# The second weight sum of a seven-product (Strassen-Winograd) block: by an accumulating DMA instead of a GpSimd add

## The chip, the cores and the metric

The kernel runs on one core of one Trainium2 chip. The metric is the time of one execution on the device in microseconds (us); lower is better. Each kernel is run several times and the median is compared.

## The reference

One inference step of a four-layer network on 640 tokens (512 of a sample, 128 of a context) of width 1024. Each layer is a token mixer (gated convolution, pooling, attention, gated convolution), then a SwiGLU feed-forward part of hidden width 2816; both are modulated by vectors computed from a conditioning vector.

```python
D_MODEL, D_FF = 1024, 2816
def swiglu(h, w_in, w_out):
    g, u = jnp.split(h @ w_in, 2, axis=-1)
    return (jax.nn.silu(g) * u) @ w_out
...
for i in range(DEPTH):
    mod_p = adaln(c_ctx[None, :], ada_w[i], ada_b[i])     # (1, 1024) @ (1024, 6144), in six parts
    ...
    xp = xp + mod_p[5] * swiglu(hp, ffn_in_w[i], ffn_out_w[i])
    xs = xs + mod_s[5] * swiglu(hs, ffn_in_w[i], ffn_out_w[i])
```

All is float32.

## The kernel before

**Products.** Activations are held transposed, 128 features by 640 tokens a tile. Each float32 operand is split in two rounded parts, hi and lo, and a product is three matmuls (hi by hi, hi by lo, lo by hi). The hi part of a weight tile is written by ScalarE, the lo part (weights minus hi) by VectorE.

**Pairs of seven blocks.** A part of the feed-forward input products is not done plainly. One gate tile and one up tile of 128 outputs make a pair, and with the two halves of the 1024 inputs and the two halves of the tokens the product is a 2 by 2 by 2 block product, done with seven block products instead of eight (the scheme of Winograd's form). Each block product is 4 x 3 = 12 matmuls of 128x128 weights on 322 columns (line 806). The order of the blocks is fixed (`_order`): for pair p it is (p,1), (p-1,4), (p,5), (p,6), (p,2), (p,7), (p,3), and for the first pair of a chunk 1, 5, 2, 6, 3, 7. There are 60 such pairs, in nine chunks of 6 or 8 pairs: eight in layer 0's second chunk and six in its third, and so on in layers 1 to 3.

**The weight sums.** Four of the seven blocks have sums of weights. With G the gate tile and U the up tile, L and R the left and right halves of their inputs: block 5 is s1 = U_L + U_R, block 6 is s2 = s1 + G_L, block 3 is s4 = s2 + G_R, block 7 is s3 = U_L + G_L. Their homes are 128x512 tiles of 256 KB: s1 in `rope[:, 0]`, s2 in `rope[:, 1]`, s4 in `tmp[:, 2]`, and s3 in the up tile's own left half. Each home holds one pair's sum at a time. For pair p the steps are, with their lines:

- SP (the queue that issues plain loads): the gate and up tiles, 512 KB each (465), issued once the tiles of pair p-2 are free (VectorE's mark at 1882, behind block 4); then U_L into the s1 home (483), when VectorE has read block 5 of pair p-1 (`free(5)`) and s2 of pair p-1 has been made (482).
- GpSimd (POOL): U_R added to the s1 home by an accumulating DMA (638); G_L added to U_L by an accumulating DMA, s3 (644); s2 by a tensor_tensor add (654) when s1 has landed; s4 by a tensor_tensor add (660) when VectorE has read block 3 of pair p-1. Then the loads of modulation weights (`load_ada`, 598), 512 KB each, into one of three slots.
- ScalarE writes each block's hi part (1303) into one of four slots of `w_hi` as a block's product before it ends; VectorE writes the lo part (1878) into `w_lo`; TensorE waits for that (801).

So block (p,6) is put into its slot when block (p-1,3) is done, and TensorE comes to it three blocks later. ScalarE and VectorE work in order, and both also do the rest of the pair: ScalarE copies block 1's result (1347) and does the silu (1368), VectorE adds the partial results (1942, 1950, 1971), multiplies, and in some chunks does products of the modulation (1787), which read the tiles that `load_ada` brings.

**Around the first pair of a chunk.** The sums of pair 0 of a chunk are made while the output products of the chunk before still run (`outs_and_first_pair`). There GpSimd's queue holds: three triples of modulation loads, the four sum steps of pair 0, one more triple, and then the sums of pair 1. This order is there in four chunks. VectorE does six modulation products of each triple in these stretches.

Of the kernel before, what the change touches and what calls it, by code (L numbers as in the profile page):

```python
# [20 lines left out]
ALU = mybir.AluOpType  # L21
# [83 lines left out]
HW = HALF * P  # L105
# [64 lines left out]
def _pairs_before(layer, c):  # L170
    return LAYER_S[layer] + sum(SEVENS[FIRST_SEVEN[layer]:c])
# [19 lines left out]
def build(nc, d):  # L191
    with ExitStack() as ctx:
# [3 lines left out]
        def sem(name):  # L196
            return ctx.enter_context(nc.semaphore(name))
# [92 lines left out]
        t_hi_ready = sem("t_hi_ready")  # L290
        t_lo_ready = sem("t_lo_ready")
        s1_in = sem("s1_in")
        s1_made = sem("s1_made")
        s2_made = sem("s2_made")
        s3_made = sem("s3_made")
        s4_made = sem("s4_made")
# [118 lines left out]
        s1_home, s2_home, s4_home = rope[:, 0, 0:HW], rope[:, 1, 0:HW], tmp[:, 2, 0:HW]  # L415

        def block_source(p, m):

            j = 2 * (p % 2)
            return {1: raw[:, j, 0:HW], 2: raw[:, j, HW:2 * HW], 4: raw[:, j + 1, HW:2 * HW], 7: raw[:, j + 1, 0:HW],  # L420
                    5: s1_home, 6: s2_home, 3: s4_home}[m]

        def block_home(w, n, b):
            slot = SLOT[n][b]
            return w[:, slot // 2, slot % 2 * HW:slot % 2 * HW + HW]
# [17 lines left out]
        def _(sp):  # L443
# [17 lines left out]
            def load(q, tiles, units=range(4)):  # L461
                for j in units:

                    sp.wait_ge(w_lo_ready, 4 * q + (j - 3))
                    sp.dma_start(raw[:, j, 0:tiles * P], d["weights"][4 * q + j, :, 0:tiles * P]).then_inc(raw_in[j], 16)

            def load_pair(layer, c, q, p):

                first, place, j, qq = _pairs_before(layer, c), PLACE[SEVENS[c]], 2 * (p % 2), q + p // 2
                load(qq, KD, (j, j + 1))  # L470
                up_w = d["weights"][4 * qq + j + 1]

                def free(m):
                    if p:
                        sp.wait_ge(block_lo_ready, SEVEN * first + place[p - 1, m] + 1)
                    elif first:
                        sp.wait_ge(block_lo_ready, SEVEN * first)

                free(5)
                if first + p:  # L480

                    sp.wait_ge(s2_made, first + p)
                sp.dma_start(s1_home, up_w[:, 0:HW]).then_inc(s1_in, 16)

            sp.dma_start(cond_k[:], d["cond_k"]).then_inc(cond_k_in, 16)
            load_head(0)
# [33 lines left out]
            for layer in range(DEPTH):  # L520
# [43 lines left out]
                for c in range(FIRST_SEVEN[layer], 3):  # L564
                    for p in range(SEVENS[c]):
                        load_pair(layer, c, q, p)
                    q += SEVENS[c] // 2
                    if c < 2:
                        with sp.Fori(0, Q_OUT) as i:
                            load(i + q, KD)  # L570
                        q += Q_OUT
# [15 lines left out]
        def _(pool):  # L587
# [45 lines left out]
            def sums_of_pair(layer, c, p, q):  # L633

                first, place, j, qq = _pairs_before(layer, c), PLACE[SEVENS[c]], 2 * (p % 2), q + p // 2
                pairs, gate_w, up_w = first + p, raw[:, j, :], raw[:, j + 1, :]
                pool.wait_ge(s1_in, 16 * (pairs + 1))
                pool.dma_start(s1_home, d["weights"][4 * qq + j + 1, :, HW:2 * HW], accum_op=ALU.add).then_inc(s1_made, 16)
                pool.wait_ge(raw_in[j], 16 * qq + 16)
                pool.wait_ge(raw_in[j + 1], 16 * qq + 16)  # L640
                if pairs:

                    pool.wait_ge(s3_made, 16 * pairs)
                pool.dma_start(up_w[:, 0:HW], gate_w[:, 0:HW], accum_op=ALU.add).then_inc(s3_made, 16)

                def free(m):
                    if pairs:
                        pool.wait_ge(block_lo_ready, SEVEN * first + (place[p - 1, m] + 1 if p else 0))

                pool.wait_ge(s1_made, 16 * (pairs + 1))  # L650
                free(6)
                if pairs:
                    pool.wait_ge(s4_made, pairs)
                pool.tensor_tensor(s2_home, s1_home, gate_w[:, 0:HW], ALU.add).then_inc(s2_made, 1)
                pool.wait_ge(s2_made, pairs + 1)
                free(3)
                if p == 0 and c == FIRST_SEVEN[layer]:

                    pool.wait_ge(sum_ready, 2 * layer + 2)
                pool.tensor_tensor(s4_home, s2_home, gate_w[:, HW:2 * HW], ALU.add).then_inc(s4_made, 1)  # L660

            def sums_of_chunk(layer, c, q, n):

                share = IN_ADA[layer][c] if isinstance(IN_ADA[layer][c], list) else []

                def load_for(p):
                    at, end = sum(share[:p]), sum(share[:p + 1])
                    for tile in range(-(-at // 2), -(-end // 2)):
                        load_ada(_ada_at(layer, c) + tile // ADA_N, tile % ADA_N)

                load_for(0)
                for p in range(n):
                    if p or c == 0:
                        sums_of_pair(layer, c, p, q)
                    load_for(p + 1)

            def outs_and_first_pair(layer, c, q):

                outs = OUT_ADA[layer][c]
                for i in range(sum(outs)):  # L680
                    if i == outs[0] + 1:
                        sums_of_pair(layer, c + 1, 0, q)
                    ada_triple(_ada_at(layer, c, 1) + i)
                if sum(outs) <= outs[0] + 1:
                    sums_of_pair(layer, c + 1, 0, q)
# [4 lines left out]
            for layer in range(DEPTH):  # L690
                q, kind, n = LAYER_Q[layer] + Q_MIX[KIND[layer]], KIND[layer], 2 * layer + 1
                first = FIRST_SEVEN[layer]
# [556 lines left out]
        def _(act):  # L1249
# [43 lines left out]
            def block_hi(n, b, first, q):  # L1293

                p, m = ORDER[n][b]
                if m in (1, 2):
                    act.wait_ge(raw_in[2 * (p % 2)], 16 * (q + p // 2) + 16)
                elif m == 4:
                    act.wait_ge(raw_in[2 * (p % 2) + 1], 16 * (q + p // 2) + 16)
                else:  # L1300
                    done, unit = {5: (s1_made, 16), 6: (s2_made, 1), 7: (s3_made, 16), 3: (s4_made, 1)}[m]
                    act.wait_ge(done, unit * (first + p + 1))
                act.activation(block_home(w_hi, n, b), block_source(p, m), ACT.Copy).then_inc(block_hi_ready, 1)  # L1303

            def first_blocks(layer, c, q, j):

                for b in {2: (0, 1), 3: (2, 3)}[j]:
                    block_hi(SEVENS[c], b, _pairs_before(layer, c), q)
# [22 lines left out]
            def seven_chunk(layer, c, q, n, r, g, tiles):  # L1331
# [8 lines left out]
                def refill(p, m):  # L1340
                    for b in REFILL[n][place[p, m]]:
                        block_hi(n, b, first, q)
# [412 lines left out]
        def _(dve):  # L1755
# [74 lines left out]
            def scaled_out(q, j, row, off_s=0, off_p=TS):  # L1830

                slot = j % 2
                dve.tensor_copy(bias[:, j, :], ps[:, 2 * slot + 1, T - TA:TH - TA])
                if off_p == off_s + TS:
                    v = dve.tensor_tensor(halves(row[:, off_s:off_s + T]), both(slot), halves(rinv), ALU.mult)  # L1835
                else:
                    for (_, src, dst), (_, _, r) in zip(pieces(slot, row, off_s, off_p), pieces(slot, rinv)):
                        v = dve.tensor_tensor(dst, src, r, ALU.mult)
                v.then_inc(freed[slot], 1)

                dve.wait_ge(freed[slot], evacuated(q, j))
# [818 lines left out]
```

## Time and profile before

| what | value |
|---|---|
| median of 3 runs | 2601.7 us (2601.56 to 2602.37) |
| time of the profiled execution | 2599.65 us |
| span in its profile (first to last instruction) | 2597.9 us |
| mean granted TensorE clock | 0.997 of full |
| busy: TensorE, VectorE, ScalarE, GpSimd | 99%, 79%, 39%, 21% |
| mean DMA traffic | 132 GB/s |

Busy time is the share of the span in which an engine executes; a TensorE that is busy is not necessarily at its peak. The profiled execution takes 1.75 us beyond its span, and is 2.05 us under the median of the runs.

### The profile page before, as it was taken

The page shows a single profiled execution, that of the slowest core. Times are in us where ns is not written, and L with a number is a line of the kernel's source. Part 1 is how long each engine was busy: PE and PEld are TensorE (multiplying, and loading weights), DVE is VectorE, ACT ScalarE, POOL GpSimd, SP SyncE. Part 2 cuts the span into 40 slices and gives each one's busy share as a digit, 9 for nine tenths or more (in the row PEclk, how much of TensorE's full clock was granted, in tenths as well). Part 3 has the DMA queues.
Part 4 walks back from the last instruction along what each step waited for, and adds up shares of the span by engine and source line. Part 5 has one row for each costly group of instructions (what it writes and reads, how often), then busy time and mean ns, then how long its engine had stood idle before and what let it go on. Part 6 is the DMA issues. An engine that isn't in the chain of part 4 may idle for free. (4 is left out here: it accounts for less than half of the span.)

```text
span 2597.9 us, 44163 instructions
## 1 busy us (share of the span) xinstructions
PE 2559.6 (99%) x16918; PEld 2485.7 (96%) x16918; DVE 2053.2 (79%) x3489; ACT 1010.1 (39%) x1687; POOL 548.3 (21%) x553
## 2 busy tenths in 40 slices
PE   9999999999999999999999999999999999999998
PEld 5999999999999999999976999999999998999998
DVE  5888879988786787987766788887788988858385
ACT  4223322533442222254676453442532234425253
POOL 0000243313100032330000531322200035223030
PEclk9999999999999999999999999999999999999999
DMA  7444335655423443542101255554534423545342
GB/s 299 153 139 146 124 112 180 173 186 146 139 77 129 147 154 121 184 128 96 58 13 41 78 132 188 144 166 142 147 110 145 149 102 109 160 112 141 98 134 78
DMA packets 111582, 342.83 MB, mean 132 GB/s; under 512 B 12993, under 2 KB 16193, under 8 KB 111169
## 3 DMA queue, kind: packets, MB, share of 16 engines
q1 hardware_dynamic: 68656, 216.48, 24.1%
q0 software_dynamic: 42768, 124.28, 17.8%
q8 instruction: 97, 1.59, 0.2%
q14 instruction: 61, 0.49, 0.1%
HBM read 322.09 MB, written 2.88 MB: 125 GB/s over the span
## 5 line engine op out<-in xcount | busy, mean ns | idle before, releaser
L1252 ACT ACTIVATE w_hi<-raw 128x1024 fp32r<-128x1024 f32 (+2 forms) x239 | 244.5, 1023 | 652.4 <-PE ps L754 625.1
L1787 DVE CUSTOM_DVE_ANT_0 ps_x<-ada_w,cond 128x1024 f32<-128x1024 f32 x354 | 453.2, 1280 | 20.8 <-DVE tmp L1835 3.7
L1759 DVE TENSOR_TENSOR w_lo<-raw,w_hi 128x1024 fp32r<-128x1024 f32 (+2 forms) x239 | 295.4, 1236 | 205.3 <-ACT w_hi L1252 203.8
L806 PE MATMUL ps<-turned,w_hi 128*128 128x322 f32 x1440 | 323.5, 312 | 9.4 <-DVE tmp L1971 5.7
L598 POOL DMA_DIRECT2D ada_w<-in_ada_w x177 | 95.4, 540 | 1061.2 <-DVE ada_raw L1787 1022.8
L753 PE MATMUL ps<-h_hi,w_hi 128*128 128x320 f32 x928 | 291.6, 314 | 3.0 <-DVE w_lo L1759 1.2
L754 PE MATMUL ps<-h_lo,w_hi 128*128 128x322 f32 x928 | 289.1, 311 | 0.0
L754 PE MATMUL ps<-h_hi,w_lo 128*128 128x322 f32 x928 | 288.4, 311 | 0.0
L753 PE MATMUL ps<-h_lo,w_hi 128*128 128x320 f32 x928 | 288.3, 311 | 0.0
L753 PE MATMUL ps<-h_hi,w_lo 128*128 128x320 f32 x928 | 288.2, 311 | 0.0
L754 PE MATMUL ps<-h_hi,w_hi 128*128 128x322 f32 x928 | 287.6, 310 | 0.0
L753 PE MATMUL ps<-g_hi,w_hi 128*128 128x320 f32 x884 | 274.1, 310 | 3.5 <-DVE g_lo L1773 3.5
L754 PE MATMUL ps<-g_hi,w_lo 128*128 128x320 f32 x884 | 273.2, 309 | 0.0
L753 PE MATMUL ps<-g_hi,w_lo 128*128 128x320 f32 x884 | 273.2, 309 | 0.0
L754 PE MATMUL ps<-g_lo,w_hi 128*128 128x320 f32 x884 | 273.1, 309 | 0.0
L754 PE MATMUL ps<-g_hi,w_hi 128*128 128x320 f32 x884 | 273.1, 309 | 0.0
L753 PE MATMUL ps<-g_lo,w_hi 128*128 128x320 f32 x884 | 273.1, 309 | 0.0
L1878 DVE TENSOR_TENSOR w_lo<-raw,w_hi 128x512 fp32r<-128x512 f32 x240 | 189.9, 792 | 88.8 <-ACT w_hi L1303 85.8
L806 PEld LDWEIGHTS ps<-turned,w_hi 128*128 128x128 f32 x1440 | 243.1, 189 | 11.5 <-DVE tmp L1971 7.3
L806 PE MATMUL ps<-h_hi,w_hi 128*128 128x322 f32 x720 | 226.2, 314 | 11.0 <-DVE w_lo L1878 11.0
L806 PE MATMUL ps<-h_hi,w_lo 128*128 128x322 f32 x720 | 225.3, 313 | 0.0
L806 PE MATMUL ps<-h_lo,w_hi 128*128 128x322 f32 x720 | 224.9, 312 | 0.0
(239 smaller groups left out, 6145.2 us busy)
## 6 DMA issues: line engine op xcount, KB each, us to landing
raw<-in_weights SPq DMA_DIRECT2D x323, 512.0 KB, 3.6
ada_w<-in_ada_w POOLq DMA_DIRECT2D x177, 512.0 KB, 3.6
rope<-in_weights SPq DMA_DIRECT2D x60, 256.0 KB, 3.5
rope<-in_weights POOLq DMA_DIRECT2D x60, 256.0 KB, 3.7
raw<-raw POOLq DMA_DIRECT2D x60, 256.0 KB, 4.6
raw<-in_weights SPq DMA_DIRECT2D x32, 384.0 KB, 3.2
mix<-in_ada_head SPq DMA_DIRECT2D x16, 512.0 KB, 10.5
x<-in_x SPq DMA_DIRECT2D x8, 320.0 KB, 10.1
```

Of the source, the lines that this page charges most:

```text
L598: pool.dma_start(ada_w[:, j * D:(j + 1) * D], d["ada_w"][ADA_N * qa + (j - LEAD)]).then_inc(ada_in[j], 16)
L753: pe.matmul(ps[:, 2 * slot, 0:TA], w[:, slot, ws], a(k)[:, 0:TA], start=begin, stop=end)
L754: mm = pe.matmul(ps[:, 2 * slot + 1, 0:width - TA], w[:, slot, ws], a(k)[:, TA:width], start=begin, stop=end)
L806: mm = pe.matmul(out, w[:, ws], a[:, k, :], start=begin and k == 0 and i == 0, stop=k == HALF - 1 and i == 2, skip_group_check=True)
L1252: act.activation(w_hi[:, j % 2, 0:tiles * P], raw[:, j, 0:tiles * P] if src is None else src, ACT.Copy).then_inc(w_hi_ready, 1)
L1759: dve.tensor_tensor(w_lo[:, j % 2, 0:tiles * P], raw[:, j, 0:tiles * P] if src is None else src, w_hi[:, j % 2, 0:tiles * P].bitcast(F32), ...
L1787: dve.tensor_tensor_reduce(ada_products, ada_w[:, j * D:(j + 1) * D], cond[:, v, :], 1.0, 0.0, ALU.mult, ALU.add, ada_raw[:, j, v:v + 1]). ...
L1878: dve.tensor_tensor(block_home(w_lo, n, b), block_source(p, m), block_home(w_hi, n, b).bitcast(F32), ALU.subtract).then_inc(block_lo_ready, 1)
```

## The change

The second sum s2 is no longer made by the GpSimd add of line 654. SP now loads G_L from HBM a second time, into the s2 home, with a plain DMA of 256 KB; GpSimd then issues a DMA from the s1 home to the s2 home, with accumulation, and waits for its landing before the add of s4. SP's new load stands behind the load of the s1 home, with two waits of its own: VectorE has read block 6 of pair p-1, and s4 of pair p-1 has been made. `s2_made` counts in steps of 16, as a DMA's landing does.

```diff
@@ load_pair, SP
                 if first + p:
-                    sp.wait_ge(s2_made, first + p)
+                    sp.wait_ge(s2_made, 16 * (first + p))
                 sp.dma_start(s1_home, up_w[:, 0:HW]).then_inc(s1_in, 16)
+                free(6)
+                if first + p:
+
+                    sp.wait_ge(s4_made, first + p)
+                sp.dma_start(s2_home, d["weights"][4 * qq + j, :, 0:HW]).then_inc(s2_in, 16)
@@ sums_of_pair, GpSimd
                 pool.wait_ge(s1_made, 16 * (pairs + 1))
-                free(6)
-                if pairs:
-                    pool.wait_ge(s4_made, pairs)
-                pool.tensor_tensor(s2_home, s1_home, gate_w[:, 0:HW], ALU.add).then_inc(s2_made, 1)
-                pool.wait_ge(s2_made, pairs + 1)
+                pool.wait_ge(s2_in, 16 * (pairs + 1))
+                pool.dma_start(s2_home, s1_home, accum_op=ALU.add).then_inc(s2_made, 16)
+
+                pool.wait_ge(s2_made, 16 * (pairs + 1))
                 free(3)
@@ block_hi, ScalarE
-                    done, unit = {5: (s1_made, 16), 6: (s2_made, 1), 7: (s3_made, 16), 3: (s4_made, 1)}[m]
+                    done, unit = {5: (s1_made, 16), 6: (s2_made, 16), 7: (s3_made, 16), 3: (s4_made, 1)}[m]
```

## Rows read from the trace of the kernel before

**Rows 1.** Busy time and share of the span, instructions, from the page.
```profile
PE 2559.6 (99%) x16918; PEld 2485.7 (96%) x16918; DVE 2053.2 (79%) x3489; ACT 1010.1 (39%) x1687; POOL 548.3 (21%) x553
```

**Rows 2.** Chain of waits of TensorE: releaser, us in total, times, longest.
```profile
PE ps L806 <- DVE w_lo L1878: 11.0, 5, 3.4
PE ps L806 <- DVE tmp L1971: 5.7, 6, 1.6
PE ps L806 <- ACT tmp L1347: 3.7, 2, 2.3
```

**Rows 3.** Busy time in one chunk of pairs (start:end, length, engines, clock, DMA).
```profile
core 0: us, PE busy (x) PEld busy (x) DVE busy (x) ACT busy (x) POOL busy (x), PEclk, DMA share, GB/s
2306.00:2404.00 98.00, 98.00 (x661) 98.00 (x660) 79.13 (x131) 50.40 (x97) 33.12 (x28) 1.00 0.49 132
```

**Rows 4.** Line 654: duration ns min/median/max, and who waited for it.
```profile
L654 POOL TENSOR_TENSOR rope<-rope,raw x60: 1267/1294/2366, 428.4 to 2527.1; 128x512 f32<-128x512 f32 x60
...
  ACT w_hi L1303: 4.1, 5
```

**Rows 5.** DMA issues of the page: KB each, median us to landing.
```profile
ada_w<-in_ada_w POOLq DMA_DIRECT2D x177, 512.0 KB, 3.6
rope<-in_weights POOLq DMA_DIRECT2D x60, 256.0 KB, 3.7
raw<-raw POOLq DMA_DIRECT2D x60, 256.0 KB, 4.6
```

**Rows 6.** Line 483, the load of the s1 home: its landing.
```profile
DMA to landing us min/median/max: 2.5/3.5/5.3
```

**Rows 7.** Timeline of a pair inside a chunk: start us, us, instruction, idle before.
```profile
471.51 0.33 SPq L483 DMA_DIRECT2D rope<-in_weights  x1
475.44 0.86 POOL L638 DMA_DIRECT2D rope<-in_weights  x1 [3.97 <-DMA rope<-in_weights]
475.98 1.21 POOL L644 DMA_DIRECT2D raw<-raw  x1
479.20 1.28 POOL L654 TENSOR_TENSOR rope<-rope,raw 128x512 f32<-128x512 f32 x1 [2.01 <-DMA rope<-in_weights]
480.55 1.62 POOL L660 TENSOR_TENSOR tmp<-rope,raw 128x512 f32<-128x512 f32 x1
482.21 0.63 ACT L1303 ACTIVATE w_hi<-rope 128x512 fp32r<-128x512 f32 x1 [1.15 <-PE ps L806]
484.46 0.57 PE L806 MATMUL ps<-turned,w_hi 128*128 128x322 f32 x2 [0.50 <-DVE tmp L1971]
486.71 0.68 DVE L1878 TENSOR_TENSOR w_lo<-rope,w_hi 128x512 fp32r<-128x512 f32 x1
```

**Rows 8.** Timeline of a pair whose first sum lands late.
```profile
1541.50 0.95 SPq L465 DMA_DIRECT2D raw<-in_weights  x2
1542.76 1.51 POOL L654 TENSOR_TENSOR rope<-rope,raw 128x512 f32<-128x512 f32 x1 [2.13 <-DMA rope<-in_weights]
1544.36 0.63 ACT L1303 ACTIVATE w_hi<-rope 128x512 fp32r<-128x512 f32 x1 [0.96 <-POOL rope L654]
1550.59 0.32 PE L806 MATMUL ps_sum<-h_hi,w_hi 128*128 128x322 f32 x1
```

**Rows 9.** DMA issues between 1538 and 1550 us: KB each, median us to landing.
```profile
raw<-in_weights SPq DMA_DIRECT2D x2, 512.0 KB, 5.3
raw<-raw POOLq DMA_DIRECT2D x2, 256.0 KB, 5.5
```

**Rows 10.** Timeline around the first two pairs of a chunk.
```profile
592.75 1.50 POOL L654 TENSOR_TENSOR rope<-rope,raw 128x512 f32<-128x512 f32 x1 [6.10 <-DMA rope<-in_weights]
594.33 2.17 POOL L660 TENSOR_TENSOR tmp<-rope,raw 128x512 f32<-128x512 f32 x1
596.43 1.14 POOL L598 DMA_DIRECT2D ada_w<-in_ada_w  x2
601.34 1.22 DVE L1787 CUSTOM_DVE_ANT_0 ps_x<-ada_w,cond 128x1024 f32<-128x1024 f32 x1
607.78 2.37 POOL L654 TENSOR_TENSOR rope<-rope,raw 128x512 f32<-128x512 f32 x1 [2.02 <-DMA rope<-in_weights]
609.21 2.03 DVE L1787 CUSTOM_DVE_ANT_0 ps_x<-ada_w,cond 128x1024 f32<-128x1024 f32 x1
613.86 0.39 PE L806 MATMUL ps<-h_hi,w_hi 128*128 128x322 f32 x1 [1.89 <-DVE w_lo L1878]
```

More of the change, by code:

```diff
@@ L292, in build @@
         s1_in = sem("s1_in")
+        s2_in = sem("s2_in")
         s1_made = sem("s1_made")
```

## The prediction

> **What bounds the kernel now.** I read the page's busy shares first: TensorE is busy for 2559.6 us of the span of 2597.9 [rows 1], so all its idle time together is 38 us. Next the waits by engine. Of TensorE's waits, those inside the chunks of pairs (line 806) are three rows: 11.0 us for VectorE's lo parts, 5.7 us for VectorE's line 1971, 3.7 us for ScalarE's copy [rows 2]. That is 20.4 us, and it caps what any relief of the engines around the pairs can give; the rest of the time TensorE streams. The busy time by stretch shows the pace there: 661 matmuls in 98 us with no gap [rows 3], 0.1483 us each, so a block of 12 takes 1.78 us and a pair of seven blocks 12.45 us. Whatever serves a pair in less is hidden; a cycle of loads and sums that took longer would set the pace instead.
>
> Then the timelines, to see how near the sums are to that. In a usual pair [rows 7] the s1 home is loaded at 471.51, the right half is accumulated from 475.44, s1 is there at 479.20, s2 at 480.5, and ScalarE takes s2 at 482.21: 1.7 us of room. VectorE takes it only at 486.71, since it is behind with other work. In a pair whose s1 lands late [rows 8] the room is gone: s1 is there at 1542.76, ScalarE has been waiting 0.96 us when it takes s2 at 1544.36. TensorE starts block 2 at 1550.59, so block 6 starts one block earlier, at 1548.81. The view by line says how many pairs are like this: ScalarE waited for line 654 in 5 of 60, 4.1 us [rows 4].
>
> **The part removed.** 60 adds of 1.29 us in the median [rows 4] leave GpSimd, which is busy 21% and is no bound by itself. What they cost is on VectorE: a modulation product takes 1.22 us at 601.34 with GpSimd quiet, and 2.03 us at 609.21 beside the add that began at 607.78 [rows 10]: 0.81 us lost. That counts only where TensorE then waits for VectorE. Four chunks begin with such a wait right behind the add of their second pair (the one shown is 1.89 us at 613.86; the other three are of the same kind, and these four make most of the 11.0 us [rows 2, 10]): 4 x 0.8 = 3.2 us gained. Inside the first chunk, where VectorE is never idle for long, three small waits for line 1971, the first 0.50 us long [rows 7], together 1.3 us, should vanish. The larger waits for 1971 (5.7 less 1.3, 4.4 us [rows 2]) stand beside the add of s4, which stays. Gain so far: 4.5 us.
>
> The trace agrees with the Trainium skill, SBUF — State Buffer, section Who interferes with whom, by which a VectorE instruction with two inputs in SBUF and a GpSimd instruction that reads SBUF share a read interface, and whichever starts second waits for the whole of the first. By that rule the loss next to one add could be up to the add's whole 1.29 us, and the four places would give 5.2 us and not 3.2; the row of 0.81 stands in my sum.
>
> **The part added on GpSimd.** One accumulating DMA of 256 KB from SBUF to SBUF a pair, and GpSimd waits for its landing. Its nearest relative is s3's, same size, same kind, 4.6 us in the median, but that one is issued 0.54 us behind another accumulating DMA [rows 5, 7] and lies in its queue; the one from HBM takes 3.7 [rows 5]. The new one is issued when s1 has just landed, with s3's nearly done, so without other traffic I take 4.0 us. Where SP's two loads of 512 KB fall on it, as at 1541.50 just ahead of 1542.76 [rows 8], landings are 5.3 and 5.5 us [rows 9], and I take 5.3. Bounds: 2.5 us, the least that a transfer of 256 KB took [rows 6], and 5.5 us. So s2 is made 2.7 to 4.0 us later than by the add (4.0 or 5.3 less 1.3).
>
> The Trainium skill, DMA: Bandwidth & Descriptors, section Anatomy of one DMA, gives 2.0 us plus the bytes over 436 GB/s, which is an estimate of 2.6 us here; the rows of this case, 3.7 and 4.6 us, lie above it. By 2.6 us neither late fills nor late modulation loads (below) would remain, and the sum would be the gain of 4.5 us alone; this is the first rival's condition.
>
> Who waits for s2? (a) ScalarE's fill of block 6, and in its queue behind it the copy of block 1, the next fills and the silu. In the usual pair the fill moves from 482.21 to 483.2, and VectorE comes at 486.71 anyway: nothing. In a late pair, 1542.76 + 5.3 + 0.63 (ScalarE) + 0.68 (VectorE, as in [rows 7]) = 1549.4, against TensorE's 1548.8: 0.6 us late. Five such pairs [rows 4]: 3.0 us. At 4.0 us of landing they would be in time by 0.7 us. (b) SP's load of the next s1 home, discussed below. (c) GpSimd's own queue: the add of s4 moves back 2.7 us (its block comes three blocks after block 6, 5 us: hidden), and so do the modulation loads behind it. Inside a chunk a tile is loaded a pair ahead, hidden. Behind the first pair of four chunks it is not: the add of s4 would end at 592.75 + 4.0 + 2.17 = 598.9, the first load of the triple, 3.6 us [rows 5], would land at 602.5, and VectorE wants it at 601.34 [rows 10]. Before, it was issued at 596.43 and landed at about 600. VectorE loses 1.2 us there with no idle time to catch up before TensorE's wait at 613.86: 4 x 1.2 = 4.8 us, which eats the 3.2 us gained at the same places. Were the landing 2.5 us, this term would be nothing; at 5.3 it would be 4 x 2.5 = 10 us.
>
> **The part added on SP.** 60 plain loads of 256 KB, 3.5 us to landing in the median, 5.3 at most [rows 6]. In SP's queue it waits for s4 of the pair before; behind it stand the loads of the next pair's tiles, which wait for a mark that comes later in any case. In the pair shown, s4 of the pair before would be ready at about 474, the load issued then lands at about 477.5, and GpSimd wants it at 479.20 [rows 7]: hidden, with 1.7 us of cover. If that cover went, each microsecond would be added to s2. Its data shares the engines with the accumulation into s1 issued at about the same time: between 0 and 0.9 us on it (rows 9 against rows 5: 5.5 less 4.6); I take it as hidden in the room of (a), except as the loop rival.
>
> **The sum.** -3.2 - 1.3 + 3.0 + 4.8 = +3.3 us on the profiled execution's 2599.65, 2602.95. That execution is 2.05 us under the median, so 2605.0 us.
>
> **Rivals.** First, faster: the DMA lands in 3 us or less, and what counts is VectorE's relief. Then -4.5 us, and if half of the other 4.4 us of waits for 1971 goes too, -6.7: 2595.0. For it: the least landing of 2.5 us, VectorE busy without a break where TensorE waits. Against: no accumulating transfer in rows 5 is under 3.7. It is faster once the two losses together are under 0 to 1 us.
>
> Second, the loop: s2 of pair p-1 releases the load of s1 of pair p, and from there it is 3.93 us to the accumulation, 3.76 to s1 [rows 7], and the new DMA. Before, this loop was 3.93 + 3.76 + 1.3 = 9.0 us, far under 12.45. Now it is 11.7 us with a landing of 4.0 and 13.0 with 5.3. If the two alternate and the extra traffic adds 0.45 us, half of the 0.9, the mean is 11.7 + 0.65 + 0.45 = 12.8 us, 0.35 over TensorE's pace; over the 50 or so pairs that aren't first in a chunk that is 17 us: 2601.7 + 17 = 2619. It decides from a mean landing of 4.8 us without further traffic. Against it: a later s1 load falls into a quieter stretch and lands sooner, which holds the loop down. If each landing were 5.3 and the traffic cost the full 0.9, it would be 1.45 x 50 = 72 us, and 2674; nothing shows all pairs meeting that.
>
> Third, the stalls of the main case are bigger, without the loop: late fills hold up ScalarE's queue behind them (copy of block 1, silu) so that each of the five costs double, +3.0, and the first-pair loss is with a landing of 4.6, +2.4: 2610.4.
>
> Fourth, the change does not relieve VectorE, since the add of s4 only moves to where other work of VectorE lies, and the late fills are covered: all terms near nothing, 2601.7.
>
> **How the numbers follow.** A measurement of this kernel can tell about 0.2%, 5.2 us, from no change: faster is under 2596.5, slower over 2606.9. Chances: main case 0.36, fourth 0.16, first 0.14, third 0.14, loop 0.20. Of the first, 0.12 falls under 2596.5. Of the main case 0.07 falls over 2606.9, with nearly all of the third and the loop. So faster 0.12, same 0.48, slower 0.40. The predicted time is the main case's, 2605.0. The range leaves out the far side of the first case and the upper half of the loop: 2595 to 2622.
>
> **What the profile after would show.** Line 654 as a DMA issue, landing near 4.0 us in the median and 5.3 where SP's loads fall on it. VectorE's busy time lower by some 30 to 50 us (60 x 0.5 to 0.8). The modulation product that stood at 601.34 waiting about 1 us for a DMA. ScalarE's fill of block 6 waiting for the DMA in many pairs, but TensorE waiting for lo parts only in about five new places, of 0.6 us each. The three small waits for 1971 in the first chunk gone. SP's load of s1 released by the new DMA in many pairs; if TensorE then waits once in every pair or two of a chunk, it is the loop. A landing over 4.8 us in the mean, or under 3, would make the prediction wrong.

## The result

The changed kernel takes 2624.1 us in the median of 5 runs (2615.7 to 2636.0), against 2601.7 before (5 runs, 2601.6 to 2608.6): a ratio of 1.0081, 95% interval 1.0062 to 1.0099. It is slower by 0.8%, 22 us, where the prediction said 2605.0 with a range up to 2622.

The profiled execution took 2627.2 us, 27.6 us over the one of before, with a span of 2625.5. In the page of the changed kernel, TensorE is busy longer [rows 1], by 9.2 us, though it executes the same matmuls, and VectorE for 34.8 us less; the new DMA's median landing is 4.0 us.

```profile
PE 2568.8 (98%) x16918; PEld 2493.3 (95%) x16918; DVE 2018.4 (77%) x3489; ACT 1004.4 (38%) x1687; POOL 495.0 (19%) x553
...
rope<-in_weights SPq DMA_DIRECT2D x120, 256.0 KB, 3.3
rope<-in_weights POOLq DMA_DIRECT2D x60, 256.0 KB, 3.7
raw<-raw POOLq DMA_DIRECT2D x60, 256.0 KB, 4.6
rope<-rope POOLq DMA_DIRECT2D x60, 256.0 KB, 4.0
```

The waits of TensorE (against [rows 2]; line 811 is the former 806, 1883 the former 1878) show where the idle time came: lo parts of weights, 29.0 us in 14 waits instead of 11.0 in 5.

```profile
PE ps L811 <- DVE w_lo L1883: 29.0, 14, 4.2
PE ps L811 <- ACT tmp L1352: 5.0, 2, 2.6
PE ps L758 <- DVE g_lo L1778: 4.8, 2, 3.0
PE ps L811 <- DVE tmp L1976: 3.5, 4, 1.9
```

TensorE's idle time went from 2597.9 - 2559.6 = 38.3 us to 2625.5 - 2568.8 = 56.7, 18.4 us more, and its busy time by 9.2: that is the 27.6 us. Of the 14 waits in the timeline, four are the old long ones behind the first two pairs of a chunk (4.05, 2.66, 4.20 and 2.62 us, 13.5 together against 10.2), and ten are new ones at block 6, 15.5 us together.

Not all of the 27.6 us belongs to the change. The 4.8 us for line 1778 are two waits, one of 1.72 and one of 3.03 us, where the kernel before had two of 1.7. The same kind of wait at 390 us of the span, before the first weight sum is made, is 3.0 us in the profiles of five of the experiments below and 0.9 or 1.7 in others, so these 1.3 us, and the lower clock of about 1.7 us beside them, can come without the change.

The view by line of the new DMA (line 658) says who waited. Where ScalarE had waited for s2 in 5 pairs [rows 4], it does so in 21, for 89.0 us.

```profile
  POOL tmp L665: 210.8, 58
  ACT w_hi L1308: 89.0, 21
...
DMA to landing us min/median/max: 3.2/4.0/7.0
```

One of the ten new waits in the timeline, in a pair with no modulation loads:

```profile
2408.87 0.86 POOL L658 DMA_DIRECT2D rope<-rope  x1 [3.34 <-DMA rope<-in_weights]
2408.95 0.80 SPq L466 DMA_DIRECT2D raw<-in_weights  x2
2409.32 0.63 ACT L1308 ACTIVATE w_hi<-rope 128x512 fp32r<-128x512 f32 x1 [1.14 <-PE ps L811]
2415.88 1.27 POOL L665 TENSOR_TENSOR tmp<-rope,raw 128x512 f32<-128x512 f32 x1 [6.15 <-DMA rope<-rope]
2415.89 0.63 ACT L1308 ACTIVATE w_hi<-rope 128x512 fp32r<-128x512 f32 x1 [5.94 <-DMA rope<-rope]
2416.56 1.15 DVE L1883 TENSOR_TENSOR w_lo<-rope,w_hi 128x512 fp32r<-128x512 f32 x1 [4.04 <-ACT w_hi L1308]
2417.85 0.54 PE L811 MATMUL ps<-turned,w_hi 128*128 128x322 f32 x2 [1.43 <-DVE w_lo L1883]
```

The DMA for s2 goes out at 2408.87; 0.08 us later SP issues the two tile loads of the next pair. The sum is there only at 2415.88, 7.0 us after its issue. ScalarE, which had filled block 5 at 2409.32 and would have taken s2 next, has waited 5.94 us; VectorE has waited for ScalarE, and TensorE for VectorE. VectorE's lo part takes 1.15 us here, beside GpSimd's add of s4, which starts at the same landing; in [rows 7] it took 0.68. In all ten new waits it takes 1.14 to 1.17 us, and TensorE starts 2.0 to 2.1 us after the landing.

I sorted the 60 pairs by the time from the DMA's issue to the start of the s4 add, against the nearest issue of a tile load. In 20 pairs a tile load is issued within 0.6 us of the DMA, before or after, and that time is 4.8 to 7.1 us, median 5.7. Fifteen of these have both loads of a pair beside them, median 6.2; the other five are first pairs with one load of 512 KB, 5.0 to 5.7. In the 27 pairs with the nearest tile load about 2 us after it or later, it is 3.3 to 5.2, median 3.4. In the ten pairs of the new waits it is 5.3 to 7.1, and nine of them are among the fifteen.

The second rival's loop has a share too. This is a pair of the first chunk, the one that [rows 7] shows before the change:

```profile
467.90 0.87 POOL L658 DMA_DIRECT2D rope<-rope  x1 [2.16 <-DMA rope<-in_weights]
474.55 0.33 SPq L484 DMA_DIRECT2D rope<-in_weights  x1
482.57 0.86 POOL L658 DMA_DIRECT2D rope<-rope  x1 [3.44 <-DMA rope<-in_weights]
489.58 1.26 POOL L665 TENSOR_TENSOR tmp<-rope,raw 128x512 f32<-128x512 f32 x1 [6.15 <-DMA rope<-rope]
491.54 0.53 PE L811 MATMUL ps<-turned,w_hi 128*128 128x322 f32 x2 [2.32 <-DVE w_lo L1883]
```

The DMA of 467.90 met tile loads and landed 6.6 us later; only then, at 474.55, could SP load the s1 home for the next pair. So the next DMA went out at 482.57, 6.65 us before TensorE was ready for its block 6 (491.54 less the wait of 2.32). Before the change the add of this pair began 8.94 us before block 6 (479.20 and 488.14, counting TensorE's matmuls by twelve). A landing of 6.9 us and 2.05 us of filling would just about have fitted into 8.94, so nearly all of the wait of 2.32 us is these 2.3 us. 2.0 of them are the late s1 load (14.7 us before block 6, where it was issued 16.6 us before it), and 0.3 the slower transfers behind it. The pair at 2408.87 is like it: its s1 load went out at 2400.97, when the sum before had landed at 2400.91. Against TensorE that is 0.75 us later than before the change, and the transfers behind it took 1.1 us more. At the wait of 1.89 us at 506.10 the s1 load was 0.4 us late. So the loop has a part in 3 of the ten new waits, about 3 of their 15.5 us.

The granted clock by stretch accounts for the other 9 us. The rows of before and of after for the same stretch:

```profile
450.00:460.00 10.00, 8.15 (x44) 7.91 (x45) 9.93 (x19) 4.32 (x9) 2.66 (x2) 0.83 0.39 134
```

```profile
450.00:460.00 10.00, 8.61 (x41) 8.38 (x42) 9.93 (x20) 4.05 (x10) 2.13 (x3) 0.70 0.52 146
```

The third number from the end is the granted clock: 0.83 and 0.70 of the full 2.4 GHz, a mix of its two levels, after TensorE had waited 3.30 us before and 4.05 us after the change. Going by such stretches of 10 us from 400 us on, and leaving out the end of the run, three of before are under 1.00, all at 0.83, with TensorE's waits of 3.30, 3.44 and 2.30 us at their edges; beside its waits of 1.9 us or shorter there is none. After the change there are ten under 1.00. They lack 15.4 us of full clock where the three lacked 5.1, and TensorE's busy time has grown by 9.2. Waits of TensorE of 1.89, 2.05, 2.41 us and longer stand beside them, but not every longer wait has one: those of 2.63 us at 1528.93 and 2.62 us at 1669.39 have none.

### The profile page after: what moved, and what is told of

It reads as the page before. It is cut to its first block and busy times, and to the rows that moved or that the text cites. A ratio compares the mean times of both kernels' runs of the same rounds, so it can differ in the third digit from the quotient of the medians.

```text
span 2625.5 us, 44283 instructions
## 1 busy us (share of the span) xinstructions
PE 2568.8 (98%) x16918; PEld 2493.3 (95%) x16918; DVE 2018.4 (77%) x3489; ACT 1004.4 (38%) x1687; POOL 495.0 (19%) x553
## 5 line engine op out<-in xcount | busy, mean ns | idle before, releaser
L1792 DVE CUSTOM_DVE_ANT_0 ps_x<-ada_w,cond 128x1024 f32<-128x1024 f32 x354 | 443.6, 1253 | 26.7 <-issue 5.9
L811 PE MATMUL ps<-turned,w_hi 128*128 128x322 f32 x1440 | 325.6, 313 | 24.0 <-DVE w_lo L1883 15.5
L811 PE MATMUL ps<-h_hi,w_hi 128*128 128x322 f32 x720 | 227.8, 316 | 13.5 <-DVE w_lo L1883 13.5
L1883 DVE TENSOR_TENSOR w_lo<-raw,w_hi 128x512 fp32r<-128x512 f32 x240 | 174.1, 726 | 84.0 <-ACT w_hi L1308 79.0
```

Source lines behind the costliest of these rows:

```text
L811: mm = pe.matmul(out, w[:, ws], a[:, k, :], start=begin and k == 0 and i == 0, stop=k == HALF - 1 and i == 2, skip_group_check=True)
L1792: dve.tensor_tensor_reduce(ada_products, ada_w[:, j * D:(j + 1) * D], cond[:, v, :], 1.0, 0.0, ALU.mult, ALU.add, ada_raw[:, j, v:v + 1]). ...
L1883: dve.tensor_tensor(block_home(w_lo, n, b), block_source(p, m), block_home(w_hi, n, b).bitcast(F32), ALU.subtract).then_inc(block_lo_ready, 1)
```

## The experiments

All compare with runs of the kernel before on the same chip, and the chip is not the same in all experiments; a ratio is the one on record with its 95% interval, which can differ by up to 0.0014 from the quotient of the two medians. Line numbers shift between kernels.

**The load alone.** GpSimd's add is back, SP's second load stays.

```diff
                 pool.wait_ge(s2_in, 16 * (pairs + 1))
-                pool.dma_start(s2_home, s1_home, accum_op=ALU.add).then_inc(s2_made, 16)
+                pool.tensor_tensor(s2_home, s1_home, gate_w[:, 0:HW], ALU.add).then_inc(s2_made, 16)
```

> s2 is again made by GpSimd's add (which now overwrites the home), but SP's second load of the gate block stays, with its waits; GpSimd waits for it before the add. Theory A (the landing of the new DMA, stretched to 6 or 7 us where SP's two tile loads are issued beside it, delivers s2 late): the load alone costs little, 2601 to 2605. Rival B (the extra 15.7 MB from HBM and SP's waits slow the other transfers): most of the 22 us remains, 2615 or more.

2606.4 us against 2607.2, ratio 1.000 (0.999 to 1.0009). The extra 15.7 MB and SP's two waits cost nothing that can be measured (at most 0.1%). Rival B falls.

**The DMA alone.** The home is loaded once, before the first pair; later pairs add to what is there. SP's two waits for the home go to GpSimd, ahead of its DMA.

```diff
-                free(6)
-                if first + p:
-
-                    sp.wait_ge(s4_made, first + p)
-                sp.dma_start(s2_home, d["weights"][4 * qq + j, :, 0:HW]).then_inc(s2_in, 16)
+                if first + p == 0:
+                    sp.dma_start(s2_home, d["weights"][4 * qq + j, :, 0:HW]).then_inc(s2_in, 16)
...
-                pool.wait_ge(s2_in, 16 * (pairs + 1))
+                pool.wait_ge(s2_in, 16)
+                free(6)
+                if pairs:
+                    pool.wait_ge(s4_made, pairs)
```

> The accumulating DMA makes s2, but the home is begun with a gate block only once, before the first pair; later pairs add to what is there (leaves out 59 of the 60 loads). Theory A: the stretched landings stay, since the tile loads still come beside the DMA, and so does most of the loss: 2613 to 2625. Rival B: near 2602 to 2606.

2636.9 us against 2607.2, ratio 1.0128 (1.0104 to 1.0151): the whole loss and somewhat more, 30 us where 11 to 23 were expected. The landing is much as in the changed kernel, and TensorE's waits too.

```profile
DMA to landing us min/median/max: 3.2/3.9/7.2
```

```profile
PE ps L811 <- DVE w_lo L1883: 31.1, 17, 4.2
```

**Tile loads after the sum.** SP's wait for s2 of the pair before stands ahead of the tile loads too.

```diff
+                if first + p:
+                    sp.wait_ge(s2_made, 16 * (first + p))
                 load(qq, KD, (j, j + 1))
```

> SP issues the two tile loads of the next pair only when s2 of the pair before has landed, so they no longer fall on the new DMA. Theory A: the landing of line 658 is 4.0 us with few above 5, TensorE's waits for lo parts of block 6 go, and the time is 2600 to 2608, unless the tiles themselves now come late. Rival C (the loss is the closed loop s2 to s1 load to s1 to s2 at its normal landing of 4.0 us, collisions or not): 2615 or more.

2657.4 us, ratio 1.0198 (1.0181 to 1.0215). Half of the expectation came: with the tile loads out of its way the DMA lands in 3.3 us in the median. The time got worse. The s1 load now stands right behind the tile loads. It lands in 4.7 us in the median, where it took 3.3 in the changed kernel.

```profile
481.63 0.86 POOL L660 DMA_DIRECT2D rope<-rope  x1 [2.23 <-DMA rope<-in_weights]
484.96 1.46 POOL L667 TENSOR_TENSOR tmp<-rope,raw 128x512 f32<-128x512 f32 x1 [2.47 <-DMA rope<-rope]
```

```profile
484.90 0.80 SPq L466 DMA_DIRECT2D raw<-in_weights  x2
485.79 0.38 SPq L486 DMA_DIRECT2D rope<-in_weights  x1
```

s2 is made 3.3 us after 481.63, the tile loads go out at 484.90, the s1 load behind them, and the next s1 accumulation begins at 492.90, 7.1 us after the s1 load where [rows 7] had 3.9. So the loop of the prediction's second rival can be made to bind by putting a collision into it; this run does not say how far it binds in the changed kernel.

**First pairs only.** A pair is by DMA if `by_dma` says so, else by the add (with a semaphore of its own); here `p == 0`, nine pairs.

```diff
+                if by_dma(layer, c, p):
...
+                    pool.dma_start(s2_home, s1_home, accum_op=ALU.add).then_inc(s2_made, 16)
...
+                else:
...
+                    pool.tensor_tensor(s2_home, s1_home, gate_w[:, 0:HW], ALU.add).then_inc(s2_added, 1)
```

> Only the first pair of each of the nine chunks is by DMA (and its extra load); the other 51 by the add. It isolates the late modulation loads behind the first pair. My prediction's term: 4.8 us, so 2606.5. If that stretch is covered after all: 2602.

2619.7 us against 2607.2, ratio 1.0045 (1.0028 to 1.0061): half of the change's loss from nine pairs, and 12.5 us where 4.8 or nothing were expected. The timeline at the place of [rows 10]:

```profile
599.10 0.87 POOL L678 DMA_DIRECT2D rope<-rope  x1 [6.73 <-DMA rope<-in_weights]
604.00 1.29 POOL L690 TENSOR_TENSOR tmp<-rope,raw 128x512 f32<-128x512 f32 x1 [4.04 <-DMA rope<-rope]
605.25 1.66 POOL L622 DMA_DIRECT2D ada_w<-in_ada_w  x3
...
621.26 0.39 PE L836 MATMUL ps<-h_hi,w_hi 128*128 128x322 f32 x1 [3.60 <-DVE w_lo L1915]
```

The landing is 4.9 us, not 4.0, the modulation loads leave 6.2 us after the DMA's issue where they left 3.7 us after the add's start, and TensorE's wait is 3.60 us instead of 1.89. The four waits of this kind are 4.74, 3.60, 5.13 and 3.35 us, 6.6 us more than before. TensorE's busy time is 2569.8 us, 10.2 more. The granted clock is under 1.00 beside all four, where before it was so beside two of them. It is so too beside two waits of 3.0 us for line 1810 (1.7 before), one of them at 392 us, ahead of all sums, so not all of the 10.2 us belongs to the first pairs.

**First pairs, with the modulation loads ahead of the wait.** GpSimd issues two loads of the triple between the DMA and the add of s4.

```diff
-                        sums_of_pair(layer, c + 1, 0, q)
-                    ada_triple(_ada_at(layer, c, 1) + i)
+                        sums_of_pair(layer, c + 1, 0, q, lambda: (load_ada(qa, 0), load_ada(qa, 1)))
+                        load_ada(qa, 2)
```

> First pairs alone by DMA, as in the run before, but GpSimd issues the first two loads of the modulation triple between the DMA and the add of s4, so they don't stand behind its landing. If the loss of 0.45% is those loads coming late: within 0.1% of before, with the granted clock back at 0.997. If it is anything else of the first pair's DMA (the load of the home, traffic): 0.3% or more stays.

2604.4 us against 2602.3, ratio 1.0006 (0.9996 to 1.0016). The four waits are 3.51, 2.13, 3.53 and 1.67 us, 0.6 us more than before in all. So the loss of the first pairs is the late modulation loads behind GpSimd's wait; what any other part of their DMA costs is 0.16% at most.

**All but the first pairs.** `p > 0`, 51 pairs.

> The first pair of each chunk goes back to the add, the other 51 are by DMA. If the two losses add up, the change's 0.8% less the 0.45% of the run with first pairs alone: about 0.35 to 0.5% over before. The late fills of block 6 stay (about ten waits of TensorE of 1 to 2 us), the waits at 451, 622, 1126 and 1669 fall back to those of before or under.

2615.7 us against 2602.3, ratio 1.0053 (1.0031 to 1.0076). With the first pairs' 0.45% that makes 0.98%, against 0.81% for both at once. There are five new waits at block 6, 9.0 us, where about ten were expected. The four old waits are 2.42, 1.10, 2.63 and 0.80 us, each 0.8 to 0.9 us under those of before: the relief of VectorE at the second pair, as the prediction priced it.

**Half the tile loads.** The whole change, but from the third pair of a chunk on SP loads left halves only (leaves out 2 x 256 KB a pair).

```diff
-                load(qq, KD, (j, j + 1))
+                load(qq, HALF if p > 1 else KD, (j, j + 1))
```

> The whole change, but SP loads only the left halves of the gate and up tiles for every pair from the third of a chunk on (leaves out 2 x 256 KB a pair; blocks 2, 4 and 3 work on stale right halves). Theory A (the tile loads beside it stretch the DMA): the landing of line 658 stays under 5.5 us, the late fills of block 6 go or shrink, and the time is that of the run with first pairs alone, +0.4 to +0.5%. Rival C (the closed loop at 4.0 us): as the change, +0.8%.

2608.9 us against 2602.3, ratio 1.0017 (1.0007 to 1.0026). The landing is 3.6 us in the median and 5.7 at most; of the ten waits at block 6 one is left, of 0.51 us. The loop is still closed here, through the same waits (SP's s1 load waited for the DMA 25 times, 31 in the changed kernel), so rival C, the loop at a normal landing, falls. But halved tile loads also shorten the other transfers in the loop, so this run doesn't separate the collision from the loop that collisions stretch. The loss is less than the +0.4 to +0.5% expected. The waits behind the first two pairs remain (2.43, 2.44, 4.45 and 2.49 us, 1.6 more than before in all); they don't account for all of the 4 to 7 us.

**The s1 load ahead of the tile loads.**

```diff
-                load(qq, KD, (j, j + 1))
...
                     sp.wait_ge(s2_made, 16 * (first + p))
                 sp.dma_start(s1_home, up_w[:, 0:HW]).then_inc(s1_in, 16)
+                load(qq, KD, (j, j + 1))
```

> The whole change, but SP issues the load of the s1 home ahead of the two tile loads, so the tile loads wait until s2 of the pair before has landed (through the wait of the s1 load), and the s1 load does not stand behind them. Theory A with the loop: the loop is about 3.3 + 3.5 + 4 = 11 us, under 12.45, the landings are 3.3 us, and only the first pairs' loss stays: +0.3 to +0.5%. If the tiles come late instead, waits of TensorE for lo parts of blocks from raw: +1% or more.

2629.8 us, ratio 1.0101 (1.0084 to 1.0118), against the expected +0.3 to +0.5%. The median landing is 3.3 us as expected, yet TensorE waits 33.2 us for lo parts in 17 waits. Twelve of them, 25.7 us, stand at block 6, and the others at blocks 3 and 7 of a first pair, as before; none is at a block from the tiles, so the second expectation fails as well in its mechanism. The longest are in the last pair of a chunk, as here:

```profile
531.52 0.95 SPq L466 DMA_DIRECT2D raw<-in_weights  x2
532.86 0.85 POOL L649 DMA_DIRECT2D raw<-raw  x1 [5.14 <-issue]
534.55 0.86 POOL L657 DMA_DIRECT2D rope<-rope  x1 [0.84 <-DMA rope<-in_weights]
540.65 1.26 POOL L664 TENSOR_TENSOR tmp<-rope,raw 128x512 f32<-128x512 f32 x1 [5.24 <-DMA rope<-rope]
542.61 0.54 PE L810 MATMUL ps<-turned,w_hi 128*128 128x322 f32 x2 [4.32 <-DVE w_lo L1882]
```

GpSimd's DMA for s3, which needs the tiles, goes out only at 532.86, 5.1 us after its step for s1, and the one for s2 waits behind it; then it meets the loads of the output products' tiles, which no wait of a pair holds back, and lands in 6.1 us. The late tiles are what it waited for: the second tile load of its pair, issued at 524.46, landed at 532.32. The view of SP's tile loads (line 466) has GpSimd's s3 step waiting for them in 52 pairs:

```profile
  POOL raw L649: 168.8, 52
```

**Second pairs only.** `p == 1`, nine pairs.

> Only the second pair of each chunk is by DMA (nine pairs), where TensorE's long waits for VectorE stood beside the add; no tile load falls there and no modulation load stands behind a late landing. The run of the inner pairs had these waits 0.8 to 0.9 us shorter each. Expected: 4 x 0.8 and 2 x 1.0 us less waiting, 5.2 us, and 1.7 us of granted clock for each of the waits that falls out of those that are followed by a lower clock: 2593 to 2597, that is 0.2 to 0.35% faster than before. If VectorE's relief isn't what shortened them: no change.

2597.7 us (11 runs) against 2601.4, ratio 0.9986 (0.9977 to 0.9995): 3.7 us faster than before, 0.14%, just short of the 0.2 to 0.35% expected. The long waits for lo parts go down [rows 2], but two waits for line 2008 (the former 1971) have grown to 2.3 us and take part of it back.

```profile
PE ps L836 <- DVE tmp L2008: 7.6, 6, 2.3
PE ps L836 <- DVE w_lo L1915: 7.4, 4, 3.0
PE ps L836 <- ACT tmp L1384: 3.4, 2, 1.7
```

**Pairs 1, 2, 4 and 6.**

> DMA in the pairs 1, 2, 4 and 6 of each chunk, the add in 0, 3, 5 and 7. Before, the pairs in which ScalarE waited for s2 were pairs 3 and 5 of their chunks. If a late sum has to meet a pair without room, and two DMA pairs in a row drag the next one along: no late fills, as e9 or up to 0.1% better. If the collision with the tile loads hurts wherever it falls: 0.1 to 0.4% slower than e9.

2601.1 us against 2601.4, ratio 1.0001 (0.9992 to 1.001), 0.15% over the second pairs alone, though the two intervals touch. The profile has one new wait at block 6, of 2.33 us.

**First and second pairs, modulation loads ahead.** `p == 1 or (p == 0 and c > 0)`: the second pairs, and the first pairs of every chunk but a stage's first, with the modulation loads moved as above.

> The second pairs by DMA, and the first pairs too where modulation loads follow, with these loads issued ahead of the wait. By the run of the split (+0.06%) the first pair's DMA brings nothing: within 0.1% of e9.

2597.5 us, ratio 0.9986 (0.9977 to 0.9995), as the second pairs alone.

**Pairs 3 and 5 only.** 18 pairs, each between two made by the add.

> Only pairs 3 and 5 of each chunk (18 pairs) by DMA, each between two pairs made by the add, so no late sum hands its lateness to the next through the load of the s1 home. These include the five pairs without room. If the collision with the tile loads alone makes the late fills: waits for lo parts of block 6 of 1 to 2 us in several of these pairs, 0.2 to 0.4% over before. If it takes the chain (a late sum, hence a late s1 load, hence the next sum on top of the next tile loads): few late fills of at most 0.6 us, within 0.15% of before.

2640.8 us against 2606.9, ratio 1.0135 (1.0117 to 1.0153): more than the whole change, from 18 of its 60 DMAs, and far over both expectations. The landing:

```profile
DMA to landing us min/median/max: 3.3/6.5/7.5
```

```profile
PE ps L836 <- DVE w_lo L1915: 37.8, 22, 3.7
```

```profile
509.05 0.85 SPq L479 DMA_DIRECT2D raw<-in_weights  x2
509.14 0.86 POOL L678 DMA_DIRECT2D rope<-rope  x1 [2.16 <-DVE w_lo L1915]
516.19 1.26 POOL L690 TENSOR_TENSOR tmp<-rope,raw 128x512 f32<-128x512 f32 x1 [6.20 <-DMA rope<-rope]
518.15 0.54 PE L836 MATMUL ps<-turned,w_hi 128*128 128x322 f32 x2 [1.69 <-DVE w_lo L1915]
```

With the sum before it on time, the DMA goes out within 0.1 us of the tile loads and takes 7.0 us. Of the 22 waits, 13 stand at block 6, 24.8 us together. No chain of late sums is needed for the collision. In the whole change the same 18 pairs have a median landing of 5.1 us: there the first tile load comes 0.55 us after the DMA in the median, and here 0.14 us before it. What shifts the two against each other was not tested.

**Pairs 3 and 5, half the tile loads.** As above, with left halves only from the third pair on (leaves out 2 x 256 KB a pair).

> As the run with pairs 3 and 5 by DMA, but SP loads only the left halves of the tiles from the third pair of a chunk on (leaves out 2 x 256 KB a pair; blocks 2, 3 and 4 work on stale right halves). If the tile loads stretch the DMA: its median landing falls from 6.5 to under 5.5 us and the loss from 1.35% to 0.4% or less. If it is something else of these pairs: 6 us or more, and 1% or more.

2604.3 us against 2601.4, ratio 1.0008 (0.9998 to 1.0018).

```profile
DMA to landing us min/median/max: 3.2/4.3/7.1
```

Halving the bytes of the tile loads takes the loss from 1.35% to 0.08%, and the median landing from 6.5 to 4.3 us. Single landings of 7.1 us remain, of which I don't know what makes them.

## Why the prediction was wrong

**The direction** of the main case and most of its structure held: slower, by late fills of block 6 and by late modulation loads, with relief at the second pairs.

**The step that failed** is the term "Five such pairs: 3.0 us", in all its factors. Its landing of 5.3 us was read off rows that show other DMAs beside tile loads [rows 9]; the new one took 5.7 us in the median with a tile load within 0.6 us, 6.2 with both loads of a pair, and up to 7.1. From the landing to TensorE it allowed 0.63 + 0.68 = 1.3 us, and each of the ten waits shows 2.0 to 2.1. And it counted only the five pairs that had no room before: three of them wait now (1.54, 2.02 and 0.99 us), and seven others do. Measured: ten waits, 15.5 us, for 3.0. The prediction named the tile loads as the neighbour to fear, but treated them as a matter of the tight pairs; with pairs 3 and 5 alone by DMA, a tile load is issued within a microsecond of the sum's DMA in 13 of the 18 pairs. It also left the loop out of this term, where it brings three of the ten sums 0.4 to 2.0 us closer to TensorE's block.

**The first pairs.** The late modulation loads were right as a mechanism (moved ahead of the wait, their loss is gone) and too small: 1.2 us at each place with a landing of 4.0, 1.7 us in the run with first pairs alone, where the landing is 4.9. Beside the 0.8 us of relief at the second pair that makes +3.3 us at the four places in the changed kernel, where the sum had 4.8 - 3.2 = 1.6.

**The relief** of 0.8 us at each of four second pairs was right: with first pairs by the add these waits are 0.8 to 0.9 us shorter. VectorE's busy time fell by 34.8 us, in the 30 to 50 foretold. Of the small waits in the first chunk those of 0.50 and 0.61 us are gone and one of 0.44 us is there, but between four new waits for block 6, 6.1 us together, they tell little. The relief agrees with the rule of the Trainium skill that the prediction cites (SBUF — State Buffer, section Who interferes with whom).

**What was missing** from the sum is TensorE's clock. 9.2 us of the 27.6 in the profile are the same matmuls taking longer, in stretches beside the longer waits. Up to about 1.7 of these are beside the 3.03 us wait that can come without the change. Most stalls of the sum should have had this second price, which could have been read from the trace of before, in the stretches around its waits of 2.3 to 3.4 us.

**The rivals.** The loop, with 2619 the nearest in time, is near in its number and right in a part of the mechanism. TensorE does not wait once in every pair or two, as it would if the loop set the pace throughout: ten pairs of 60 wait. SP's s1 load was released by the new DMA in 31 pairs, and in three of the ten that made the sum later, about 3 of 15.5 us. Pairs 3 and 5 alone lose more than the whole change without two DMAs in a row. The first rival's landing of 3 us or less never came, 3.2 is the least; its relief of VectorE without a loss came with the second pairs alone, 0.14%. Of the fourth a piece is there: the add of s4 now begins together with the lo part of the same sum where TensorE waits for it, 1.15 us for 0.68, about 0.5 us in each of the ten waits. The extra load and SP's waits were rightly costed at nothing. The estimate of 2.6 us for an unhindered landing, from the Trainium skill's page DMA: Bandwidth & Descriptors, section Anatomy of one DMA, is under the shortest measured, 3.2 us.

**What stays open:** why the DMA alone, without the second load, was no faster and rather slower than the whole change (1.0128 against 1.0081, intervals apart; by medians 1.0114 against 1.0086, on different chips), how the loop and the collisions share the loss beyond the waits read above, and the single long landings with halved tiles.

## What to carry to other kernels

A small transfer on a short path does not have a duration, it has one alone and another beside each transfer that is triggered by the same progress. Look up in the timeline what is issued within a few microseconds of the place where it would go, in each position of the loop, and price it with that neighbour's bytes ahead of it. When one in-order queue gets a wait for a DMA in place of a short instruction, move ahead of it everything that doesn't need the result, and add to each new stall of TensorE of some 2 us what the clock can take beside it. If a transfer's landing releases two engines that feed the same stall, look whether they slow each other. Where a change helps in a few places and hurts in the others, make it only there: nine of the sixty pairs gave 0.14%.

## What the runs showed of the hardware

An accumulating DMA of 256 KB from SBUF to SBUF took 3.3 us from issue to landing alone. Beside 1 MB of loads by another queue it took, up to the start of the s4 add and by the nearest of these loads: 5.9 to 7.1 us when that was issued between 0.3 us before it and 0.4 us after (nine pairs), 4.8 to 5.7 at 0.5 to 0.6 us after (six), and 4.1 to 4.4 at 0.7 to 0.9 us after (five). Loads issued just after it stretch it as much as loads issued just before.

The second load of 256 KB a pair from HBM, 15.7 MB in all, changed the time by less than can be measured (ratio 1.000, 0.999 to 1.0009).
